# Retention's chunk matmuls issued alternately on two halves of TensorE's array, and a weight split taken in two parts

## The reference, cut to what matters

```python
scores = jnp.einsum('blhd,bmhd->bhlm', qf, kf) * decay[None]
intra = jnp.einsum('bhlm,bmhe->blhe', scores, vf)
cross = jnp.einsum('blhd,bhde->blhe', qf, S_prev) * jnp.exp(...)
kdec = kf * jnp.exp(...)
S_new = jnp.exp(lg * L) * S_prev + jnp.einsum('blhd,blhe->bhde', kdec, vf)
```

## Time and profile before

| | us |
|---|---|
| median of 3 runs (2334.96 to 2335.87) | 2335.31 |
| the profiled execution, own time | 2335.35 |
| its span, first to last instruction | 2333.5 |
| TensorE's matmuls busy in the span | 2203.4 (94%) |
| VectorE, ScalarE, GpSimd busy | 986.0, 919.1, 607.9 |
| chain that ended last, TensorE's share | 32% |
| chain that ended last, GpSimd's share | 3% |

### The profile page before, as it was taken

How to read it: one execution, slowest core, us unless ns; L and a number is a source line. 1 busy time by engine, 2 the same in 40 slices (tenths; PEclk the granted TensorE clock), 3 DMA queues, 4 the chain that set the end, 5 groups by cost and what they waited for, 6 DMA issues and landing times. The chain is left out here.

```text
span 2333.5 us, 30656 instructions
## 1 busy us (share of the span) xinstructions
PE 2203.4 (94%) x11120; PEld 1786.3 (77%) x11120; DVE 986.0 (42%) x1525; ACT 919.1 (39%) x1466; POOL 607.9 (26%) x374
## 2 busy tenths in 40 slices
PE   7999999889999788999999899799999999998999
PEld 6899999667777566777777578677778888886787
DVE  3343544363663856777787610221022222223211
ACT  5333332233443333777777510442234333334100
POOL 1321121220220000556666441211132111114300
PEclk9999999999999888999999999899999999999999
DMA  5222222211201204999999654422222322224431
GB/s 158 43 56 52 68 70 59 59 37 36 64 1 46 71 33 157 346 332 329 323 328 317 218 158 145 145 77 77 77 98 93 102 87 75 76 75 125 156 108 54
DMA packets 257722, 287.94 MB, mean 123 GB/s; under 512 B 69818, under 2 KB 169084, under 8 KB 257468
## 3 DMA queue, kind: packets, MB, share of 16 engines
q1 hardware_dynamic: 240730, 252.78, 34.2%
q10 hardware_dynamic: 16866, 33.53, 3.9%
HBM read 246.03 MB, written 41.26 MB: 123 GB/s over the span
## 5 line engine op out<-in xcount | busy, mean ns | idle before, releaser
L228 PE MATMUL bank<-whi,x_hi 128*128 128x512 f32 (+1 forms) x1536 | 589.9, 384 | 19.7 <-POOL wlo L208 14.5
L230 PE MATMUL bank<-wlo,x_hi 128*128 128x512 f32 (+1 forms) x1536 | 576.5, 375 | 0.0
L232 PE MATMUL bank<-whi,x_lo 128*128 128x512 f32 (+1 forms) x1536 | 576.0, 375 | 0.0
L228 PEld LDWEIGHTS bank<-whi,x_hi 128*128 128x128 f32 x1536 | 290.0, 189 | 82.4 <-POOL wlo L208 24.5
L261 ACT ACTIVATE projected<-bank 128x512 f32<-128x512 f32 (+1 forms) x160 | 92.2, 576 | 600.8 <-PE bank L232 572.0
L232 PEld LDWEIGHTS bank<-whi,x_lo 128*128 128x128 f32 x1536 | 290.3, 189 | 41.6
L230 PEld LDWEIGHTS bank<-wlo,x_hi 128*128 128x128 f32 x1536 | 290.8, 189 | 38.7 <-issue 0.7
L2232 POOL TENSOR_TENSOR dec_v_lo<-dec_v,dec_v_hi 128x1024 fp32r<-128x1024 f32 x86 | 220.4, 2581 | 191.0 <-ACT dec_v_hi L2589 191.0
L208 POOL TENSOR_TENSOR wlo<-wraw,whi 128x512 fp32r<-128x512 f32 (+1 forms) x184 | 221.7, 1237 | 27.8 <-ACT whi L200 27.8
L2404 DVE TENSOR_TENSOR dec_kt_lo<-bank,dec_kt_hi 128x512 fp32r<-128x512 f32 x256 | 168.4, 683 | 82.0 <-ACT dec_kt_hi L2579 81.2
L2579 ACT ACTIVATE dec_kt_hi<-bank 128x512 fp32r<-128x512 f32 x256 | 144.5, 593 | 106.8 <-PE bank L2260 106.0
(11 more groups left out here) (373 smaller groups left out, 3405.2 us busy)
## 6 DMA issues: line engine op xcount, KB each, us to landing
dec_k<-cache_k SPq DMA_DIRECT2D x256, 256.0 KB, 3.9
dec_v<-cache_v SPq DMA_DIRECT2D x256, 256.0 KB, 4.2
wraw<-w_in_even SPq DMA_DIRECT2D x32, 512.0 KB, 6.9
wraw<-w_in_odd SPq DMA_DIRECT2D x16, 1024.0 KB, 8.7
gv<-projected ACTq DMA_DIRECT2D x4, 2304.0 KB, 8.0
gm_v<-gv SPq DMA_DIRECT2D x8, 1152.0 KB, 6.0
m<-gm_mt ACTq DMA_DIRECT2D x8, 1056.0 KB, 4.0
out_wraw<-w_out_odd SPq DMA_DIRECT2D x16, 512.0 KB, 5.2
```

Of the source, the lines that this page charges most:

```text
L228: pe.matmul(bank[:, 0:width], e.xhi[:, k, c:c + P], e.whi[:, k, 0:width], start=(k == 0), stop=False)
L230: pe.matmul(bank[:, 0:width], e.xhi[:, k, c:c + P], e.wlo[:, k, 0:width], start=False, stop=False)
L232: mm = pe.matmul(bank[:, 0:width], e.xlo[:, k, c:c + P], e.whi[:, k, 0:width], start=False, stop=(k == KD - 1))
```

## The change

The keys and queries that are turned, and the states, get 128 partitions. Chunks 1 to 4 keep the lower 64; chunks 5 to 8 lie in the upper 64. So the four chunks of the second half contract over rows 64 to 127 of the array in `scores` and in the state part of `out`, and write to PSUM partitions 64 to 127 in `add_states`. In each of the three steps the matmuls are issued alternately, first half, second half. In `out` the sixteen weighted-value matmul passes of both halves come first, then the state passes of both. VectorE and ScalarE do the same copies and chain steps on the new partitions (the fourth state is written across, from the lower partitions to the upper). At the start of layer 1 ScalarE does four of the eight pieces of the first weights between the roots of tiles 0 and 1.

```diff
-def act_split(act, e, r, width, raw=None):
+def act_split(act, e, r, width, raw=None, ks=range(KD)):
-    for k in range(KD):
+    for k in ks:
...
-    q_turned = sb("q_turned", [DK, TT, P])
-    k_turned = sb("k_turned", [DK, TT, P])
+    q_turned = sb("q_turned", [P, TT, P])
+    k_turned = sb("k_turned", [P, TT, P])
-    states = sb("states", [DK, NT, DV])
+    states = sb("states", [P, NT, DV])
...
+    def side(half):
+        return slice(DK * half, DK * half + DK)
...
         def add_states(q):
-            for half, u in enumerate(use_state):
+            for u in use_state:
                 pe.wait_ge(mb.read(u), mb.read_before(q, u))
-                for i in range(4):
+            for i in range(4):
+                for half, u in enumerate(use_state):
                     t = 4 * half + i + 1
-                    mm = pe.matmul(mb.bank(u)[0:DK, P * i:P * i + P], qk[:, t, 1, :], values(q)[:, t, :],
+                    mm = pe.matmul(mb.bank(u)[side(half), P * i:P * i + P], qk[:, t, 1, :], values(q)[:, t, :],
                                    start=True, stop=True)
-                mm.then_inc(mb.written(u), 1)
+                    if i == 3:
+                        mm.then_inc(mb.written(u), 1)
...
         def scores(q):
-                for i in range(4):
+            for i in range(4):
+                for half, u in enumerate(use_scores):
                     t = 4 * half + i + 1
-                    mm = pe.matmul(mb.bank(u)[:, P * i:P * i + P], k_turned[:, t, :], q_turned[:, t, :],
-                                   start=True, stop=True)
+                    mm = pe.matmul(mb.bank(u)[:, P * i:P * i + P], k_turned[side(half), t, :],
+                                   q_turned[side(half), t, :], start=True, stop=True)
...
         def out(q):
-                pe.wait_ge(mb.read(use_state[half]), mb.read_by(q, use_state[half]))
-                for i in range(4):
+            for u in use_state:
+                pe.wait_ge(mb.read(u), mb.read_by(q, u))
+            for i in range(4):
+                for half, u in enumerate(use_out):
                     t = 4 * half + i + 1
                     if t > 1:
-                        mm = pe.matmul(mb.bank(u)[:, P * i:P * i + P], q_turned[:, t, :], states[:, t - 2, :],
-                                       start=False, stop=(i == 3))
-                mm.then_inc(mb.written(u), 1)
+                        mm = pe.matmul(mb.bank(u)[:, P * i:P * i + P], q_turned[side(half), t, :],
+                                       states[side(half), t - 2, :], start=False, stop=(i == 3))
...
+                        ins = dve.scalar_tensor_tensor(states[side(ch > 2), ch, :], states[side(half), ch - 1, :],
+                                                       gamma[side(half), 2 * q:2 * q + 1], part, ALU.mult, ALU.add)
...
                     opening.root(act, 0)
+                    act_split(act, ev, 0, VW, raw_first, range(0, KD // 2))
                     opening.root(act, 1)
                     opening.hi(act, 0)
-                    act_split(act, ev, 0, VW, raw_first)
+                    act_split(act, ev, 0, VW, raw_first, range(KD // 2, KD))
```

More of the change, by code:

```diff
@@ L734, in scores @@
             alone(pe, e)
-            mm = pe.matmul(mb.bank(u)[0:NS, 0:NS], k_turned[:, 0, 0:NS], q_turned[:, 0, 0:NS],
+            mm = pe.matmul(mb.bank(u)[0:NS, 0:NS], k_turned[0:DK, 0, 0:NS], q_turned[0:DK, 0, 0:NS],
                            start=True, stop=True)
@@ L859, in attend @@
             dve.wait_ge(mb.written(u), mb.written_by(q, u))
-            dve.tensor_copy(k_turned[:, 1:5, :], mb.bank(u)[DK:2 * DK, :].rearrange("p (t c) -> p t c", t=4))
-            dve.tensor_copy(q_turned[:, 1:5, :], mb.bank(u)[0:DK, :].rearrange("p (t c) -> p t c", t=4)).then_inc(
+            dve.tensor_copy(k_turned[0:DK, 1:5, :], mb.bank(u)[DK:2 * DK, :].rearrange("p (t c) -> p t c", t=4))
+            dve.tensor_copy(q_turned[0:DK, 1:5, :], mb.bank(u)[0:DK, :].rearrange("p (t c) -> p t c", t=4)).then_inc(
                 mb.read(u), 1)
@@ L864, in attend @@
             dve.wait_ge(mb.written(u), mb.written_by(q, u))
-            dve.tensor_copy(k_turned[:, 0, 0:NS], mb.bank(u)[DK:2 * DK, 0:NS])
+            dve.tensor_copy(k_turned[0:DK, 0, 0:NS], mb.bank(u)[DK:2 * DK, 0:NS])
             for parity in range(2):
                 dve.tensor_copy(q_both[DK * parity:DK * parity + DK, :], mb.bank(u)[0:DK, 0:NS])
-            dve.tensor_copy(q_turned[:, 0, 0:NS], mb.bank(u)[0:DK, 0:NS]).then_inc(mb.read(u), 1)
+            dve.tensor_copy(q_turned[0:DK, 0, 0:NS], mb.bank(u)[0:DK, 0:NS]).then_inc(mb.read(u), 1)
             dve.wait_ge(mb.read(u), mb.read_by(q, u))
@@ L878, in attend @@
                     ch = 4 * half + i
-                    part = mb.bank(u)[0:DK, P * i:P * i + P]
+                    part = mb.bank(u)[side(half), P * i:P * i + P]
                     if ch == 0:
-                        ins = dve.tensor_copy(states[:, 0, :], part)
+                        ins = dve.tensor_copy(states[0:DK, 0, :], part)
                     else:
-                        ins = dve.scalar_tensor_tensor(states[:, ch, :], states[:, ch - 1, :],
-                                                       gamma[0:DK, 2 * q:2 * q + 1], part, ALU.mult, ALU.add)
+                        ins = dve.scalar_tensor_tensor(states[side(ch > 2), ch, :], states[side(half), ch - 1, :],
+                                                       gamma[side(half), 2 * q:2 * q + 1], part, ALU.mult, ALU.add)
                     if i < 3:
@@ L1001, in turned @@
             act.wait_ge(mb.written(u), mb.written_by(q, u))
-            act.activation(k_turned[:, 5:9, :], mb.bank(u)[DK:2 * DK, :].rearrange("p (t c) -> p t c", t=4),
+            act.activation(k_turned[DK:2 * DK, 5:9, :], mb.bank(u)[DK:2 * DK, :].rearrange("p (t c) -> p t c", t=4),
                            ACT.Copy)
-            act.activation(q_turned[:, 5:9, :], mb.bank(u)[0:DK, :].rearrange("p (t c) -> p t c", t=4),
+            act.activation(q_turned[DK:2 * DK, 5:9, :], mb.bank(u)[0:DK, :].rearrange("p (t c) -> p t c", t=4),
                            ACT.Copy).then_inc(mb.read(u), 1)
@@ L1022, in out @@
             act.dma_start(a["o_state_p"][0, 0][q:q + 1, :, :].rearrange("h d e -> d (h e)"),
-                          states[:, NT - 1, :]).then_inc(state_stored.sem, 16)
+                          states[DK:2 * DK, NT - 1, :]).then_inc(state_stored.sem, 16)
             for parity in range(2):
```

## The result

The changed kernel takes 2311.05 us (median of 4 runs, 2310.35 to 2311.39), the kernel before 2335.14 (4 runs, 2332.67 to 2335.87): a ratio of 0.9898, 95% interval 0.9881 to 0.9915. Predicted were 2313.2 us and a range of 2309 to 2331. The profiled execution of the changed kernel took 2310.35 us, its span 2308.6, its mean granted clock 0.978. In the rows after the change the lines are shifted: `add_states` is L722, `scores` L735, the weighted values L787, the state part of `out` L795, the sample's score L743 (L735 before); L200, L208, L228, L230, L232, L421 and L464 are unchanged.

What follows compares the result with a forecast made beforehand. TensorE was taken as the bound, with matmuls in flight for 94% of the span. From 2335.35 us, 19.7 for retention's overlap and fewer shape changes and 2.5 for layer 1's split gave 2313.2 us, range 2309 to 2331.

Steps and rivals of the forecast that it cites:

- Part 1a: In `out`, two changes of array shape fewer, 2 x 0.195 = 0.39 us a head.
- Part 1b: In `add_states`, `scores` and the state part of `out`, both halves run at once, saving 0.76, 0.78 and 0.67 us a head.
- The good end: In the three steps, passes of the two halves run side by side: 16 passes take 9 slots, 14 take 8.
- passes start in order: In the three steps, TensorE starts passes in order, the second of one half beside the first of the other.
- the first and last stand alone: In each of the three steps, the first and last passes have no partner, so n passes need n/2 + 1 slots.
- What carries through: At retention round ends GpSimd keeps 1.7 of 2.8 us spare, no new wait; before the ninth round `out`'s gain is lost.
- Part 2: At layer 1's start, splitting ScalarE's work starts GpSimd 4.3 us earlier; 2.5 us gain taken, bounds 4.3 gain to 2.3 loss.
- The sum: Whole kernel: 2335.35 - 19.7 - 2.5 = 2313.2 us, 0.95% faster.
- Only row halves: Rival: `scores` and the state part of `out` overlap, `add_states` does not; 2319.3 us, chance 0.12.
- only column halves: Rival: `add_states` overlaps, `scores` and the state part of `out` stay at 0.1115 us a pass; 2324.0 us, chance 0.13.
- No overlap: Rival: passes go one behind the other; only fewer shape changes and layer 1's split count; 2330.1 us, chance 0.15.
- Alternation paid: Rival: in the three steps each change of half costs 0.195 us like a change of shape; 2360 us, chance 0.15.

Runs made afterwards that it cites:

- the kernel on one half: Changed kernel's new matmul order and two-part split, but chunks 5 to 8 stay in the lower 64 rows and columns: 2329.62 us.
- the one in fours: Changed kernel with each step issuing four matmuls of the first half, then four of the second, instead of alternating: 2321.02 us.
- the one-bank profile: Changed kernel with both column halves of `add_states` written to one PSUM bank and the wait for the states moved before `out`: 2310.80 us.
- the last experiment: Changed kernel with ScalarE's first three pieces of the ninth round's weight split begun before the last retention tile ends: 2304.67 us.

## Why the prediction was right

**Part 1a, fewer changes of shape: right.** 0.39 us a head was forecast, and the kernel on one half shows 4.02 - 3.63 = 0.39.

**Part 1b, both halves at once: right, with one term mis-sized.** The good end was taken; rows and columns both overlap. The step that failed is "passes start in order", and with it "the first and last stand alone". In `add_states` and `scores` the first pass already has a partner 6 ns behind it (the first line of the table), and that is the other half's first pass, which stands third in the program: the two starred passes, each its half's last, pair up as well (815 and 821 ns). So 16 passes take 8 slots and not 9. That is 0.86 and 0.89 us instead of 0.76 and 0.78. In the state part, 14 passes take 8 slots as forecast, but for another reason: the first chunk has no state, so the last two passes of the second half have no partner (6 pairs and 2); that this term came out, 1.06 for `out`, is luck. Over the seven heads that carry through, the missed slots are 7 x (2.80 - 2.60) = 1.4 us.

**What carries through: right.** The 1.7 us left to GpSimd were 1.78, no wait appeared, and `out` is lost in front of the ninth round. There the profile gained 1.42 us between the starts of the ninth round and the one behind it (73.81 for 75.23) where 2.80 - 1.06 = 1.74 should be left. The difference has a place. Two more rows of the kernel before, from the timeline of TensorE:
```profile
427.68 0.63 PE L230 MATMUL bank<-wlo,x_hi 128*128 128x512 f32 x1
...
435.65 0.40 PE L230 MATMUL bank<-wlo,x_hi 128*128 128x512 f32 x1
```
and one of the changed kernel:
```profile
417.69 0.40 PE L230 MATMUL bank<-wlo,x_hi 128*128 128x512 f32 x1
```
Before, slow matmuls (0.63 us and not 0.40) began at 427.68, ahead of the last wait, which ended at 429.66, so some of the slow time lay where TensorE had to wait anyway; now no slow matmul lies ahead of the wait, and the first is the one that ends it, 411.26. From there the sixteenth matmul comes 6.43 us later instead of 5.99.

**Part 2: right in direction, mis-sized.** 2.5 us were taken of 4.3; 3.42 came. GpSimd did start 4.25 earlier. The give-back that I put at "1 to 2 us" was 0.83 (12.80 us for the eight pieces instead of 11.97).

**The sum.** 19.6 (seven heads at 2.80) + 1.4 (the eighth) + 3.4 = 24.4 us where 22.2 were forecast; the medians differ by 24.1. The missed slots and the split make up the 2.2.

**The rivals.** *Only row halves* falls by `add_states` at 1.03 us, *only column halves* by `scores` at 1.09. The Trainium skill (TensorE: Matmul & The Clock Gate, what overlaps and what doesn't) has weight loads overlap a matmul only in another row group; here it doesn't hold, since the column halves share all their rows, and their loads run beside each other and beside passes in flight (98.33 to 99.42 for `add_states`). The timelines of the weight loads, twelve of `add_states` and the sixteen of `scores`:
```profile
98.49 0.69 PEld L722 LDWEIGHTS bank<-projected,ret_qk 128*64 128x64 f32 x12
...
99.35 0.97 PEld L735 LDWEIGHTS bank<-ret_q_turned,ret_k_turned 64*128 64x128 f32 x16 [0.17 <-issue]
```
Twelve loads of 0.137 us would take 1.64 one behind the other and are done in 0.69; sixteen of 0.188 would take 3.0 and are done in 0.97 (a load is no shorter after the change: 0.136 and 0.187 on the mean). *No overlap* was priced at 2330.1; the kernel on one half, which is this case made real, took 2329.62. *Alternation paid* (0.195 us a change of half) falls by the 6 ns between the halves. The rule of the Trainium skill (TensorEngine Tiling (Array Packing), Key Properties) that different tiles load and multiply in parallel holds at every pair of the table.

What stays open: from the round behind the ninth to layer 1 the kernels differ in nothing, and yet their profiles drift by up to 3.6 us against the changed kernel's (the one in fours; the one-bank profile loses 3.3 us on the way, its median none). The slow stretches fall in other places in each; that they are the cause was not shown. What sets the place of such a stretch, and why the look-ahead ends at three passes, was not tried.

## What to carry to other kernels

Matmuls that use only 64 rows or 64 columns of the array are worth placing on both halves when TensorE is the bound (row halves, here, each with a bank of its own), and the order of issue decides how much of it comes: alternate, or go in twos, but no block longer than that. Gather them between the changes of shape, which cost 0.195 us each here. Then look for the place where a shorter stream meets a producer that hangs on something earlier: one such wait took back 1.06 us here, and starting the producer 2.6 us earlier brought the wait's end 3.7 us forward.

## What the runs showed that I had not expected

- Two passes on different halves start 6 to 7 ns apart, and from a step's second pair on the next pair follows 109 to 112 ns after it: the two share a slot from the first pass on.
- Passes do not start in the order of the program. With blocks of four, three passes of the second half start ahead of the last of the first. The Trainium skill (TensorE: Matmul & The Clock Gate, what overlaps and what doesn't) has matmuls start in program order; the starred pass at 814 ns shows that across halves they don't.
- Column halves may write the same bank of PSUM at the same time without a cost: the sixteen passes of `add_states` take 1.09 us with one bank or with two.
- A wait that ends earlier can move a stretch of slow clock as well: in the last experiment the matmuls behind it gained 1.45 us (5.13 - 3.68) that no wait accounts for.
